# Pairs within blocks of a gated linear attention: VectorE and ScalarE in place of GpSimd

## What is computed

```python
b = jnp.cumsum(gi, axis=2)            # log decays, gi <= 0
diff = b[:, :, :, None, :] - b[:, :, None, :, :]
decay = jnp.exp(jnp.where(causal[:, :, None], diff, -jnp.inf))
scores = jnp.einsum('bhik,bhjk,bhijk->bhij', qi, ki, decay)
```

## Time and profile before

| | |
|---|---|
| median of 3 runs | 1256.51 us (1255.54 to 1261.02) |
| the profiled execution | 1258.28 us, its span 1256.5 us |
| mean granted clock of TensorE | 0.954 |
| busy: PE, DVE, ACT, POOL | 1173.9, 805.2, 657.2, 306.7 us |
| the loop of the 22 steps of the third layer | about 846 to 956 us of the span |

### The profile page before, as it was taken

The page is one execution under the profiler, slowest core; times in us unless marked ns, Lnnn a source line. Parts: engine busy times, 40 slices in busy tenths (PEclk is TensorE's granted clock), DMA queues, the critical chain, the costliest instruction groups (busy, mean ns, idle before and its releaser), DMA issues.

```text
span 1256.5 us, 21300 instructions
## 1 busy us (share of the span) xinstructions
PE 1173.9 (93%) x7748; PEld 1059.7 (84%) x7748; DVE 805.2 (64%) x1292; ACT 657.2 (52%) x1095; POOL 306.7 (24%) x315
## 2 busy tenths in 40 slices
PE   8999899899999899979989999989888898999998
PEld 7998788899999799978889999978877687888776
DVE  5766555766666685665476666665945457557775
ACT  6654245645555666423465555555722545556674
POOL 2002500322222300161032222225790010012222
PEclk9999999899999999999999999989895598999999
DMA  6543103365556364400236566533321016458895
GB/s 238 169 151 118 35 1 115 105 193 184 183 184 186 101 191 146 135 34 2 88 116 192 184 184 185 182 101 117 120 100 51 1 34 223 151 183 278 313 312 182
DMA packets 49798, 181.09 MB, mean 144 GB/s; under 512 B 5568, under 2 KB 5728, under 8 KB 49600
## 3 DMA queue, kind: packets, MB, share of 16 engines
q1 hardware_dynamic: 48816, 176.98, 43.8%
q0 software_dynamic: 912, 3.16, 0.8%
HBM read 179.07 MB, written 1.05 MB: 143 GB/s over the span
## 4 chain that ended last, share of the span: by engine, by line
PE 75%; DVE 10%; ACT 5%; DMA 4%; POOL 4%; issue 1%; SPq 0%; DVEq 0%; POOLq 0%; ACTq 0%
PE bank L1626 19%; PE bank L1627 19%; PE bank L1628 19%; DMA ring<-etiles 2%; PE bank L1861 2%; PE bank L1707 2%; PE bank L1859 2%; PE bank L1850 2%; DVE wx L1421 1%; DVE w L1421 1%; PE bank L1685 1%; DMA sq<-etiles 1%; POOL region L1560 1%; POOL y L2551 1%; PE bank L1676 1%
## 5 line engine op out<-in xcount | busy, mean ns | idle before, releaser
L2204 DVE TENSOR_TENSOR w<-ring,w 128x1024 fp32r<-128x1024 f32 x234 | 289.0, 1236 | 122.3 <-ACT w L1966 122.3
L1626 PE MATMUL bank<-act,w 128*128 128x256 f32 x1216 | 353.0, 290 | 13.6 <-DVE w L2204 5.8
L1627 PE MATMUL bank<-act,w 128*128 128x256 f32 x1216 | 348.4, 286 | 0.0
L1628 PE MATMUL bank<-act,w 128*128 128x256 f32 x1216 | 347.9, 286 | 0.0
L1966 ACT ACTIVATE w<-ring 128x1024 fp32r<-128x1024 f32 x234 | 246.2, 1054 | 79.2 <-PE bank L1628 79.1
L1626 PEld LDWEIGHTS bank<-act,w 128*128 128x128 f32 x1216 | 237.5, 195 | 19.2 <-issue 14.3
L1627 PEld LDWEIGHTS bank<-act,w 128*128 128x128 f32 x1216 | 237.9, 196 | 2.0
L1628 PEld LDWEIGHTS bank<-act,w 128*128 128x128 f32 x1216 | 237.5, 195 | 0.0
L2474 DVE SCALAR_TENSOR_TENSOR region<-bank,pf,region 128x255 f32<-128x255 f32 (+1 forms) x176 | 84.8, 482 | 78.4 <-ACT region L2167 67.4
L2167 ACT ACTIVATE region<-bank,pf 128x256 f32<-128x256 f32 x88 | 49.7, 565 | 135.1 <-PE bank L1628 135.1
L2573 POOL TENSOR_TENSOR region<-region 128x256 f32<-128x256 f32 x44 | 65.2, 1481 | 183.2 <-DVE region L2474 124.9
(11 more groups left out here) (403 smaller groups left out, 2267.5 us busy)
## 6 DMA issues: line engine op xcount, KB each, us to landing
ring<-wtiles SPq DMA_DIRECT2D x234, 512.0 KB, 3.5
ring<-etiles SPq DMA_DIRECT2D x58, 512.0 KB, 5.0
sq<-etiles SPq DMA_DIRECT2D x38, 512.0 KB, 4.7
region<-packp POOLq DMA_DIRECT2D x4, 512.0 KB, 4.5
cst<-consts SPq DMA_DIRECT2D x1, 1348.0 KB, 11.9
x<-xt SPq DMA_DIRECT2D x2, 512.0 KB, 6.1
out<-x SPq DMA_DIRECT2D x4, 256.0 KB, 2.7
pa<-packa POOLq DMA_DIRECT2D x3, 285.5 KB, 5.3
```

The source lines that it names most:

```text
L1626: t.matmul(out_, still[:, 0], moving[:, 0], start=first, stop=False)
L1627: t.matmul(out_, still[:, 0], moving[:, 1], start=False, stop=False)
L1628: return t.matmul(out_, still[:, 1], moving[:, 0], start=False, stop=last)
L2204: v.tensor_tensor(w_lo[:, s, :], ring[:, s, :], w_hi[:, s, :].bitcast(F32), ALU.subtract).then_inc(lo_ready, 1)
```

## The change

`pairs_b`, new on VectorE, in step U_GOG + 2 = 8 ahead of the refill, replaces POOL's subtractions; `pairs_k`, new on VectorE, in step 14 ahead of the refill, replaces POOL's products with k; `pairs_q` stays in step 13. Each now has four instructions in place of 16: part g covers the queries 4g to 4g + 3 of all blocks with the keys 0 to 4g + 3, so it includes some pairs with the key after the query. The difference is taken the other way round (key less query), and ScalarE bounds it below by zero with a Relu before it takes Exp with scale -1, so that those pairs get exp(0) = 1; the mask gmask removes them later. ACT has eight instructions in place of one. POOL's list is then taps 0 to 23 without a break. TensorE waits for pr_ready = 4 (GB // 4) in place of 1.

```diff
@@ second_tensor
-                    pe.wait_ge(pr_ready, 1)
+                    pe.wait_ge(pr_ready, GB // 4)
@@ second_scalar
                 if u == U_PAIRS - 1:
-                    act.wait_ge(pr_sub, 1)
-                    a.activation(g_pr[:], g_pr[:], ACT.Exp).then_inc(pr_exp, 1)
+                    for g in range(GB // 4):
+                        part = g_pr[:, 4 * g:4 * g + 4, :].rearrange("p r (b j) -> p r b j", j=GB)[:, :, :, 0:4 * g + 4]
+                        act.wait_ge(pr_sub, g + 1)
+                        a.activation(part, part, ACT.Relu).then_inc(pr_pos, 1)
+                        act.wait_ge(pr_pos, g + 1)
+                        a.activation(part, part, ACT.Exp, scale=-1.0).then_inc(pr_exp, 1)
@@ second_vector
+            def pair_part(g):
+                return g_pr[:, 4 * g:4 * g + 4, :].rearrange("p r (b j) -> p r b j", j=GB)[:, :, :, 0:4 * g + 4]
+            def by_key(row, g):
+                part = row[:].rearrange("p (b j) -> p b j", j=GB)[:, :, 0:4 * g + 4]
+                return part.unsqueeze(1).to_broadcast([P, 4, NGB, 4 * g + 4])
+            def by_query(row, g):
+                part = row[:].rearrange("p (b r) -> p r b", r=GB)[:, 4 * g:4 * g + 4, :]
+                return part.unsqueeze(3).to_broadcast([P, 4, NGB, 4 * g + 4])
+            def pairs_b():
+                dve.wait_ge(gc_ready, 1)
+                dve.wait_ge(zeroed, 4)
+                for g in range(GB // 4):
+                    v.tensor_tensor(pair_part(g), by_key(g_b, g), by_query(g_b, g), ALU.subtract).then_inc(pr_sub, 1)
             def pairs_q():
-                dve.wait_ge(pr_exp, 1)
-                for r in range(GB):
-                    pr = g_pr[:, r, :].rearrange("p (b j) -> p b j", j=GB)[:, :, 0:r + 1]
-                    q_i = g_q[:].rearrange("p (b r) -> p b r", r=GB)[:, :, r].unsqueeze(2).to_broadcast([P, NGB, r + 1])
-                    ins = v.tensor_tensor(pr, pr, q_i, ALU.mult)
-                ins.then_inc(pr_q, 1)
+                for g in range(GB // 4):
+                    dve.wait_ge(pr_exp, g + 1)
+                    v.tensor_tensor(pair_part(g), pair_part(g), by_query(g_q, g), ALU.mult).then_inc(pr_q, 1)
+            def pairs_k():
+                for g in range(GB // 4):
+                    dve.wait_ge(pr_q, g + 1)
+                    v.tensor_tensor(pair_part(g), pair_part(g), by_key(g_k, g), ALU.mult).then_inc(pr_ready, 1)
...
+                if u == U_GOG + 2:
+                    pairs_b()
                 if u == U_PAIRS:
                     pairs_q()
+                if u == U_PAIRS + 1:
+                    pairs_k()
@@ second_pool
-            def pairs(other, op):
...
             taps(0, POOL_TAPS[0])
-            pool.wait_ge(gc_ready, 1)
-            pairs(g_b, decay).then_inc(pr_sub, 1)
             taps(POOL_TAPS[0], POOL_TAPS[1])
-            pool.wait_ge(pr_q, 1)
-            pairs(g_k, lambda pr, r, k_j: pl.tensor_tensor(pr, pr, k_j, ALU.mult)).then_inc(pr_ready, 1)
             taps(POOL_TAPS[1], POOL_TAPS[2])
```

More of the change, by code:

```diff
@@ L543, in block_program @@
         pr_sub, pr_exp, pr_q, pr_ready = (sem(f"pr_{n}") for n in ("sub", "exp", "q", "ready"))
+        pr_pos = sem("pr_pos")
         dg_ready = sem("dg_ready")
```

## The result

The changed kernel takes 1261.71 us (median of 14 runs, 1258.08 to 1265.95) against 1256.05 for the kernel before (14 runs, 1252.72 to 1261.02): a ratio of 1.0043, 95% interval 1.0028 to 1.0058. It is slower, by less than the 0.5% that I counted as no change. The forecast of 1252.5 is 9.2 us too low, and its range, 1248 to 1258, does not hold the time. The profiled execution took 1261.49 us, with a span of 1259.7 against 1256.5.

The account below looks back on a forecast made before the run. PE was taken as the bound, its two large third-layer waits set by VectorE and POOL; 5.4 us of delay against the removed hole and clock gave -4, from 1256.5 to 1252.5 us, range 1250.5 to 1254.5, with rivals 1248 to 1258.

Parts of the forecast that it names:

- GpSimd's chain: Third layer's POOL list: 33 us removed, last tap at 912.5, VectorE's 14.8 us wait and PE's 8.3 us gone.
- The first pass: VectorE's four wide subtractions in step 8, beside POOL's taps: 4.2 us, bounded by 3.0 and 5.2.
- the 160-element row: L1182's 160-element product, 862 ns against 322 by L1195's line: some 0.54 us for a caught operation, 5.2 a pass.
- signs of being wrong: A pass above 6 us, Relu/Exp table loads, second group earlier but span not, or a first hole that does not grow.
- From there PE runs without a wait: From tile 16 to the end of the first within-blocks group, PE never waits and all is 5.4 us late.
- Hole and clock: Around the first within-blocks group: the removed hole and clock give back 9.5 us; second group ends 4.1 us earlier.
- the same sum: Delay ahead of the first group, 5.4 us, set against what hole and clock give back: -4 us.
- ScalarE: Four Relus and four Exps from near 897 to 903: about 6.2 us, 2.6 more, covered, no table loads.
- VectorE becomes the bound of the whole stretch: Rival at steps 8 and 13: patterns at twice the element price, delay 11.2 us, 1258.2 us; chance 0.13.
- The clock did not hold: Rival judged: full clock through the first within-blocks group, second group ending 6.3 us earlier, 1250.2 us; chance 0.22.
- swallowed later: Rival: a load or the attention chain is last anyway, so the gain is lost, 1256.5 us; chance 0.10.

Follow-up runs that it names:

- e3: The changed kernel with GpSimd's 24 taps left out, a memset standing for them: 1241.57 us, ratio 0.9854 to the kernel before.
- e9: The changed kernel with the subtraction pass right ahead of the 15 products, and GpSimd pausing after 12 taps until the product with q: 1254.07 us, ratio 0.9972.
- e10: The kernel before with only the products with k moved to VectorE as four wide ones, and GpSimd's wait for q removed: 1262.07 us, ratio 1.0034.
- e6: The changed kernel with the pair work behind the first hole and GpSimd's last taps held until the products between blocks end: 1255.74 us, ratio 0.9994.

## Why the prediction was wrong, step by step

I set each start against the first gated convolution value, since the stretch began 0.6 us earlier in the changed kernel.

**GpSimd's chain: right.** It loses its 33 us, the last tap ends at 917.6 (912.5 forecast), 20 taps from 877.2 taking 2.02 us each where I had 1.74, still far ahead of VectorE's first use of it, at 941; the stall of VectorE's tap in step 18 is gone and so are PE's 8.3 us.

**The first pass: mis-sized by 0.7 us.** "I take 0.3 for each wide one, 4.2 for the pass" became 4.93. VectorE's groups by line and form, 883 to 889 us (total us and mean ns):

```profile
L1213 DVE TENSOR_TENSOR region<-region 128x1024 f32<-128x1024 f32 x1 | 1.7, 1749 | 0.0
...
L1213 DVE TENSOR_TENSOR region<-region 128x768 f32<-128x768 f32 x1 | 1.4, 1364 | 0.0
L1213 DVE TENSOR_TENSOR region<-region 128x512 f32<-128x512 f32 x1 | 1.2, 1225 | 0.0
...
L1213 DVE TENSOR_TENSOR region<-region 128x256 f32<-128x256 f32 x1 | 0.8, 825 | 0.0
```

In e3, without taps, the four took 419, 684, 949 and 1218 ns (420, 660, 910 and 1150 in the working). So each of the four is caught, for 0.4 to 0.5 us, as the 160-element row had said. I set that row aside for the splits', which then ran beside GpSimd's small operations and not beside its taps. The Trainium skill's rule ("SBUF — State Buffer", Who interferes with whom), taken strictly, gave 5.2 by the price of the 160-element row; 4.93 is nearer to it than to 4.2.

**What lay beside the pass: left out, the step that failed.** I moved every operation of VectorE after step 8 by the pass alone and kept its old price. But with GpSimd's 32 small operations and its pause went the times at which VectorE ran more cheaply. The 15 products start 8.76 us later into the stretch: 4.86 for the pass, 0.41 for ScalarE (L962), and 3.5 for what the working left at its old price: 1.0 for the splits of steps 7 to 11, at 1.63 to 1.76 where they had been 1.35 to 1.63, and 2.5 for the taps and query decays of steps 6 to 11, a pair of taps at 1.69 to 1.72 where from step 7 on it had been 1.08 to 1.71. From there to the split of tile 15, 0.93 more (0.6 to 0.9 forecast, right). From that split to the one of tile 16 it is 2.18 more: the pass with q 4.51 for 3.46, two taps 1.70 for 1.00, the split 1.63 for 1.22. The sum is 8.76 + 0.93 + 2.18 = 11.9 where the working has 5.4. None of the signs of being wrong that I had named came: they watched the moved passes, and not what stood beside them.

**"From there PE runs without a wait": wrong.** PE idles 2.50 us ahead of tile 16, and works through it at the lower of its clocks, 1.2 GHz. The windows of PE there and behind the first group (columns: window and length; busy time of PE, PEld, DVE, ACT, POOL; granted clock, DMA share, GB/s):

```profile
921.00:926.00 5.00, 5.00 (x24) 5.00 (x25) 4.96 (x8) 0.00 (x0) 0.00 (x0) 0.50 0.35 105
950.40:953.90 3.50, 3.50 (x24) 3.17 (x21) 1.04 (x3) 0.00 (x0) 0.00 (x0) 0.53 0.40 146
```

PE starts tile 16 11.6 us late. The tile takes 5.26 us at 0.50 for 2.94 before, so the delay is 14.0 us at L641 and 14.2 at the first within-blocks group.

**Hole and clock: right.** I gave them 9.5 us back by the end of the second group. That group starts 4.75 us later, not 14.2, and ends 3.9 later: 9.5 and 10.3 us back. The clock fell behind the first group as forecast, 0.53 in the second window. With 14.2 in place of 5.4, the same sum comes out at +4.7 and not at -4, which is 1261.2 in place of 1252.5; the take-out is 3.9 late, and the median 1261.71.

**ScalarE: right.** Eight operations from 901.96 to 907.6, 5.7 us (6.2 forecast), with no table load between Relu and Exp:

```profile
901.96 0.41 ACT L975 ACTIVATE region<-region 128x256 f32<-128x256 f32 x1
902.39 0.42 ACT L977 ACTIVATE region<-region 128x256 f32<-128x256 f32 x1
...
906.58 1.06 ACT L977 ACTIVATE region<-region 128x1024 f32<-128x1024 f32 x1
```

The copy and square of tile 14 are queued behind them, so PE waits 2.02 us at its lengths (L1694); that costs nothing here, since the 5.08 behind it ends with VectorE. In e9 the same queue is exposed.

**The rivals.** "VectorE becomes the bound of the whole stretch" named the place and the point from which it decides, 9.5 us of delay; its mechanism, patterns at twice the price of an element, is refuted by 3.02 for a pass without taps. The clock did not hold, and nothing was swallowed later: behind the stretch both kernels have the same 301 us to go.

**Open.** Why the kernel before has stretches of 87.3 and 85.2, and what the rest of e9's gain is (its median gained 3.2 us, its stretch 2.6 or 0.5), wasn't settled. Nor was it tried to move GpSimd's taps elsewhere for good.

## What to carry to other kernels

When work leaves an engine whose operations make those of another dearer, price not only the work: look at what the vacated time was sheltering. Take each instruction on the bound engine at its price beside the neighbour that it will have, and not the one that it had. And idle time on an engine off the path can be an asset, to be laid, with one wait, where the bound engine's most exposed operations run.

## What the runs showed of the hardware

- Sixteen small two-operand VectorE products took 3.46 us with GpSimd silent and 8.69 beside its 256-wide taps (e10); fifteen others 3.12 and 7.5 to 7.9. The price is per instruction that is caught, whatever its size: in e10 eleven of the sixteen took 0.4 to 0.6 us more than by the line through L1195's rows, the other five nothing, and of a wide pass all four were caught, for 0.4 to 0.5. So small ones suffer the most in proportion: the sixteen took 2.5 times as long, a wide pass 4.93 for 3.02.
- GpSimd pays as well: tap operations of 0.61 to 0.80 us took 1.47 to 1.60 where a VectorE operation had begun before them. In the changed kernel the one from 881.21 took 1.48 us; VectorE's split beside it ran from 880.45 to 882.21, so the tap operation ended 0.48 us after the split, as if it had stood still until then.
- The four wide operations of a pass, in runs of 4 to 16 elements with a broadcast operand, took 419 to 1218 ns for 256 to 1024 elements without taps (e3): 1.04 ns an element.
- GpSimd's small subtractions made VectorE's operations less dear than its taps did: splits of 1.35 to 1.58 us beside them against 1.63 to 1.76 beside taps without a break, and 1.21 beside nothing.
- Relu took no table load between Exps (above). In e6, where a Sqrt (L994, 899.80) had run before, Relu ran without one and the Exp behind it loaded, for 1.28 us. ScalarE's timeline of e6:

```profile
906.03 0.42 ACT L975 ACTIVATE region<-region 128x256 f32<-128x256 f32 x1 [1.64 <-DVE region L1213]
906.47 1.28 ACT L977 ACT_TABLE_LOAD   x1
```
